# Hybrid trunk kernel: the modulation row products move into the feed-forwards and the projection

## The chip, the cores and the metric

One core of a Trainium2 chip runs the whole program. The metric is the device time of one execution in microseconds (us). In the trace an f32 matmul shows as two instructions (two LDWEIGHTS and two MATMUL), a float32r matmul and a transpose as one.

## The reference

Two trunk layers over three groups of 128 tokens (one of context, two of latents, all of width 1024):

```python
silu(c) @ w_ada + b_ada -> sh1, sc1, g1, sh2, sc2, g2, sh3, sc3, g3     # per layer, c and c_ctx
h = x * (1 + sc1) + sh1;  x = layer_norm(ALPHA * x + 0.5 * g1 * swiglu(h))
h = x * (1 + sc2) + sh2;  x = layer_norm(ALPHA * x + g2 * mixer(h))      # RWKV-7 | GLA | differential attention
h = x * (1 + sc3) + sh3;  x = layer_norm(ALPHA * x + 0.5 * g3 * swiglu(h))
```

The first line is what this change is about: for each of the three sub-layers a product of the two conditioning vectors with a 1024 x 3072 matrix (12 MB in f32). Two thirds of it (shift and scale) are needed as columns before the sub-layer's input can be made, the last third (gate) as rows before its output is added.

## The kernel before

The program is written by hand for each engine. SyncE streams all weights, in chunks of 128 x 2048 f32 (1 MB), through a ring of 6 slots; `arrived[slot]` says that a chunk landed, `used` that one was freed. A chunk of feed-forward or projection weights is two units: ScalarE rounds a unit to float32r (L1428), VectorE takes the rest (L1780), and TensorE makes three products for each (L850, L853, L854), moving 384 tokens.

A layer runs `turn_x(0)`, `feed_forward(0)`, `norm(0)`, `turn_x(1)`, `project`, attention, GLA and RWKV stages, `mix_out`, `norm(1)`, `turn_x(2)`, `feed_forward(2)`, `norm(2)`. Between layers and before the long mixer stages all engines meet, and at a layer's end the semaphores are cleared (L740, L741).

A feed-forward has 22 tiles. A tile is 24 matmuls for the gate half into bank 0, 24 for the up half into bank 1 (`tile_up`, L850 to L854), and 18 of 512 columns (`tile_down`, L896) into banks 2 to 7 for the tile ahead of it. Twenty of the tiles are in loops of four. `spread_gate` (L828) makes the gate as full tiles in banks 4 to 7, and ScalarE copies it (L1434).

The row products (`row_product`, L678) have silu(c) in 32 columns as the stationary operand and the weights as the moving one, 256 columns wide. The four pairs of k write to four groups of 32 partitions of the same bank. A set is 12 chunks: chunks 0 to 7 are shift and scale, 8 to 11 the gate. Sets 1, 2 and 3 (3 for the next layer) go through the ring like all weights. Set 1 is behind feed-forward 0, set 2 behind `mix_out`, set 3 behind feed-forward 2: `modulation_rows` makes 64 products under the norm, ScalarE copies them to `mod_row` (L715), 16 matmuls with `sel` (L699) turn them to columns, VectorE adds the biases (L722, L725), and only then `turn_x` can read the banks. The 32 gate products (`gate_rows`) stand between the transposes of `turn_x` (L842), or for set 3 behind the turns; VectorE adds them to `gate_row` (L733), which GpSimd has cleared and filled with the bias behind the norm (L2300, L2303).

In the norm VectorE's last operation is L1873; x is ready with its end. GpSimd loads the layer's parameters when a layer starts (L2339 to L2344).

## Time and profile before

| | before |
|---|---|
| three runs, us | 2279.59, 2276.31, 2273.07; median 2276.31 |
| profiled execution, us | 2282.56 |
| its span, us | 2280.8, mean granted clock 0.907 |
| TensorE busy | 2007.6 us (88%), 15488 matmul instructions |
| VectorE, ScalarE, GpSimd busy | 1109.6, 707.5, 120.0 us |
| HBM read | 269.56 MB, 120 GB/s over the span |
| row products (L678) | 1152 instructions |
| loads of a layer's start | 6 chunks of 1024 KB by SyncE; GpSimd: 626, 256, 736, 256, 256 and 1024 KB |

The span is cut by stages that repeat: turn phase, feed-forward, norm, turn phase, projection, mixer stages, output projection, norm, turn phase, feed-forward, norm; the first layer ends at about 1164, the second begins at about 1175. A stage in which TensorE is busy at every moment is read by its matmuls; at the seams the question is which engine's last instruction lets the next one go.

### The profile page before, as it was taken

The page shows a single profiled execution, that of the slowest core. Times are in us where ns is not written, and L with a number is a line of the kernel's source. Part 1 is how long each engine was busy: PE and PEld are TensorE (multiplying, and loading weights), DVE is VectorE, ACT ScalarE, POOL GpSimd, SP SyncE. Part 2 cuts the span into 40 slices and gives each one's busy share as a digit, 9 for nine tenths or more (in the row PEclk, how much of TensorE's full clock was granted, in tenths as well). Part 3 has the DMA queues.
Part 4 walks back from the last instruction along what each step waited for, and adds up shares of the span by engine and source line. Part 5 has one row for each costly group of instructions (what it writes and reads, how often), then busy time and mean ns, then how long its engine had stood idle before and what let it go on. Part 6 is the DMA issues. An engine that isn't in the chain of part 4 may idle for free. (4 is left out here: it accounts for less than half of the span.)

```text
span 2280.8 us, 36833 instructions
## 1 busy us (share of the span) xinstructions
PE 2007.6 (88%) x15488; PEld 1772.9 (78%) x15488; DVE 1109.6 (49%) x1687; ACT 707.5 (31%) x1155; POOL 120.0 (5%) x104
## 2 busy tenths in 40 slices
PE   5999998996749879999969999899966598899995
PEld 3899994985639759999849999769755596599995
DVE  0434335526784764343453434454377647634345
ACT  1422223335432333222232222143444223422221
POOL 0000001000022010000010000010000410100000
PEclk8899998998569989999969999989976699799998
DMA  7533336331000173333463333453300002733320
GB/s 323 218 127 129 129 122 247 117 123 47 12 1 4 50 273 124 127 115 126 151 241 129 126 129 129 167 202 120 129 6 7 2 4 90 264 129 129 121 100 28
DMA packets 40403, 274.65 MB, mean 120 GB/s; under 512 B 4741, under 2 KB 6549, under 8 KB 8289
## 3 DMA queue, kind: packets, MB, share of 16 engines
q1 hardware_dynamic: 35280, 255.34, 30.9%
q0 software_dynamic: 2400, 11.50, 1.3%
q10 hardware_dynamic: 2608, 6.14, 0.7%
q8 instruction: 89, 1.46, 0.3%
q14 instruction: 26, 0.20, 0.0%
HBM read 269.56 MB, written 3.41 MB: 120 GB/s over the span
## 5 line engine op out<-in xcount | busy, mean ns | idle before, releaser
L1780 DVE TENSOR_TENSOR ring_r<-ring,arena_r 128x1024 fp32r<-128x1024 f32 x280 | 327.6, 1221 | 658.5 <-ACT arena_r L1428 658.3
L854 PE MATMUL bank<-arena_r,ring_r 128*128 128x384 f32 x1728 | 588.0, 340 | 0.0
L850 PE MATMUL bank<-arena_r 128*128 128x384 f32 (+1 forms) x1504 | 520.2, 346 | 17.8 <-DVE arena_r L1800 12.9
L853 PE MATMUL bank<-arena_r 128*128 128x384 f32 x1408 | 476.3, 338 | 0.0
L854 PEld LDWEIGHTS bank<-arena_r,ring_r 128*128 128x128 f32 x1728 | 327.7, 190 | 0.0
L850 PEld LDWEIGHTS bank<-arena_r 128*128 128x128 f32 x1504 | 287.5, 191 | 29.3 <-DVE ring_r L1780 16.6
L896 PE MATMUL bank<-arena_r 128*128 128x512 f32 x1056 | 300.8, 393 | 0.0
L1428 ACT ACTIVATE arena_r<-ring 128x1024 fp32r<-128x1024 f32 x280 | 276.7, 1050 | 43.9 <-PE bank L854 31.0
L1467 ACT ACTIVATE arena<-bank 128x384 f32<-128x384 f32 x88 | 43.3, 492 | 757.5 <-PE bank L854 757.5
L853 PEld LDWEIGHTS bank<-arena_r 128*128 128x128 f32 x1408 | 266.2, 189 | 4.6 <-issue 1.0
L896 PEld LDWEIGHTS bank<-arena_r 128*128 128x128 f32 x1056 | 197.5, 188 | 38.3
L896 PE MATMUL bank<-ring_r,arena_r 128*128 128x512 f32 x528 | 164.5, 392 | 0.0
L678 PE MATMUL bank<-ring,silu_c 128*32 128x256 f32 x1152 | 100.8, 496 | 51.3 <-DVE arena L1836 29.2
L1780 DVE TENSOR_TENSOR ring_r<-ring,lnrow_r 128x1024 fp32r<-128x1024 f32 x60 | 73.4, 1226 | 147.3 <-ACT lnrow_r L1428 147.2
L896 PEld LDWEIGHTS bank<-ring_r,arena_r 128*128 128x128 f32 x528 | 99.3, 188 | 22.8
L850 PE MATMUL bank<-arena_r,lnrow_r 128*128 128x384 f32 x320 | 111.6, 349 | 4.1 <-DVE ring_r L1780 4.1
L678 PEld LDWEIGHTS bank<-ring,silu_c 128*32 128x32 f32 x1152 | 39.1, 135 | 97.5 <-DVE arena L1836 31.6
L853 PE MATMUL bank<-arena_r,lnrow_r 128*128 128x384 f32 x320 | 108.0, 337 | 0.0
L1428 ACT ACTIVATE lnrow_r<-ring 128x1024 fp32r<-128x1024 f32 x60 | 63.3, 1059 | 142.5 <-PE bank L854 142.5
L2298 POOL TENSOR_TENSOR x<-x,lnrow 128x1024 f32<-128x1024 f32 x12 | 28.2, 2347 | 1362.0 <-DVE x L1859 1362.0
L853 PE MATMUL bank<-ring_r,arena_r 128*128 128x512 f32 (+1 forms) x240 | 90.4, 377 | 0.0
L1037 PE MATMUL bank<-arena 32*128 32x128 f32 x384 | 52.1, 443 | 19.5 <-DVE arena L1984 19.1
(290 smaller groups left out, 2513.4 us busy)
## 6 DMA issues: line engine op xcount, KB each, us to landing
ring<-weights SPq DMA_DIRECT2D x230, 1024.0 KB, 4.8
ring<-first_ada SPq DMA_DIRECT2D x12, 1024.0 KB, 13.6
lnrow<-ln_in POOLq DMA_DIRECT2D x6, 1024.0 KB, 7.7
const<-consts ACTq DMA_DIRECT2D x1, 2659.0 KB, 13.7
x<-x_in ACTq DMA_DIRECT2D x1, 1536.0 KB, 19.5
y_out<-x SPq DMA_DIRECT2D x3, 512.0 KB, 2.6
rows<-row_in POOLq DMA_DIRECT2D x2, 736.0 KB, 14.5
par<-par_in POOLq DMA_DIRECT2D x2, 626.0 KB, 9.1
```

What stands on the lines that cost most here:

```text
L678: mm = pe.matmul(ps[q // 2][rows_at, (q % 2) * 256:(q % 2) * 256 + 256], silu_c[:, 2 * (k % 2):2 * (k % 2) + 32], ring_tile(n0 + q)[:, k, ...
L850: mm = pe.matmul(out, w_h, h_h, start=start, stop=False, skip_group_check=True)
L853: pe.matmul(out, w_h, h_l, start=False, stop=False, skip_group_check=True)
L854: return pe.matmul(out, w_l, h_h, start=False, stop=stop, skip_group_check=True)
L896: mm = pe.matmul(ps[2 + 2 * g + n][:, :], a, w[:, n * 512:n * 512 + 512], start=(first and a is a_hi and w is hi), stop=(last and a is a_l ...
L1037: mm = pe.matmul(ps[4 * (u % 2) + h][:, t], g_qk[lo:lo + GLA_DK, u % 2, 1, t], g_qk[lo:lo + GLA_DK, u % 2, 0, t], start=True, stop=True)
L1428: sc.activation(place, unit_of(FIRST[stretch], u), ACT.Copy).then_inc(w_rounded, 1)
L1467: sc.activation(sgt[:, b, :], ps[0][:, 0:TOK], ACT.Silu).then_inc(silu_done, 1)
L1780: ve.tensor_tensor(low_unit(FIRST[stretch], u), raw, place.bitcast(F32), ALU.subtract).then_inc(w_ready, 1)
L2298: po.tensor_tensor(x[:, g, :], x[:, g, :], lnrow[:, 1, :], ALU.add).then_inc(x_ready, 1)
```

## The change

1. Set 1 rides in feed-forward 0, set 3 in feed-forward 2 of the first layer. Each chunk is made as two halves of 128 columns (`half_row`): four of them in tile 1, one ahead of the gate half of each later tile, into free columns of bank 0. ScalarE copies each (`keep_row`). One turn (`turn_row`) stands ahead of each up half, four in tile 2, into free columns of bank 1. The gate part is no longer turned but added from `mod_row` in one operation at the feed-forward's end.
2. These chunks go to two slots of their own (`ada_ring`), loaded by GpSimd's queue from an array `ada_in` (`load_rows`), ahead of the norm in its order.
3. Set 2 rides in the projection, by the order `STREAM`: its chunks stay in the ring, one behind each chunk of weights from the second on (`row_part`), with two turns behind it (`turn_part`).
4. The feed-forward loops are written out; VectorE waits for the layer's parameters ahead of feed-forward 0; the gate's bias is fetched later or earlier by GpSimd (`next_gate`).
5. In attention's scores, in GLA's products, and in RWKV's `carries`, `gains` and `outer` the order of the matmuls is changed so that neighbours use other rows of the array and other banks; the waits ahead of `carries` and `gains` are joined.

The diff, cut to its core:

```diff
+def project_stream():
+    out, q = [("feat", 0)], 0
+    for c in range(1, N_FEAT):
+        out.append(("feat", c))
+        if q < 9:
+            out.append(("ada2", q))
+            q += 1
+    for c in range(N_TOKM):
+        out.append(("tokm", c))
+        if q < N_ADA:
+            out.append(("ada2", q))
+            q += 1
+    return out
...
+                    def half_row(j, i, bank, lo):
+                        n = N_ADA * (j // 2) + i // 2
+                        if i % 2 == 0:
+                            pe.wait_ge(ada_arrived[n % ADA_SLOTS], 16 * N_ADA * l + 16 * (n // ADA_SLOTS + 1))
+                        w = ada_ring[:, n % ADA_SLOTS, :].rearrange("p (k n) -> p k n", k=KT)
+                        for k in ROW_ORDER:
+                            rows_at = slice(32 * (k // 2), 32 * (k // 2) + 32)
+                            mm = pe.matmul(bank[rows_at, lo:lo + P], silu_c[:, 2 * (k % 2):2 * (k % 2) + 32],
+                                           w[:, k, P * (i % 2):P * (i % 2) + P], start=(k % 2 == 0), stop=(k % 2 == 1),
+                                           skip_group_check=True)
+                        mm.then_inc(mod_row_mm, 1)
+                    def turn_row(part, to, i):
+                        return pe.matmul(to[:, 2 * i:2 * i + 2], part, sel[:, :, 0], start=True, stop=True,
+                                         skip_group_check=True)
...
                             mm.then_inc(turned, 1)
-                            if j > 0:
-                                gate_rows(pe, FIRST[f"ada{j}"], range(4 * k, 4 * k + 4))
...
+                        def tile_up(f):
                             u = 0 if f == 0 else 3 * f - 1
+                            if i0 + f > 0:
+                                pe.wait_ge(silu_done, i0 + f)
+                            if rides and f >= 2:
+                                pe.wait_ge(mod_row_ready, rows0 + f + EARLY_HALVES - 2)
+                                half_row(j, f + EARLY_HALVES - 2, ps[0], TOK)
+                            widen(ps[0], u, gate_mm, fresh=(f == 0))
+                            if rides and f == 1:
+                                for i in range(EARLY_HALVES):
+                                    half_row(j, i, ps[2 + i // 2], P * (i % 2))
+                            if i0 + f > 0:
+                                pe.wait_ge(act_ready, i0 + f)
+                            if rides and f >= 2:
+                                if f == 2:
+                                    for i in range(EARLY_HALVES):
+                                        turn_row(mod_row[:, i * P:i * P + P], ps[1][:, TOK:TOK + 32], i)
+                                elif f + EARLY_HALVES - 3 < 16:
+                                    i = f + EARLY_HALVES - 3
+                                    mm = turn_row(mod_row[:, i * P:i * P + P], ps[1][:, TOK:TOK + 32], i)
+                                    if i == 15:
+                                        mm.then_inc(mods_done, 1)
+                            widen(ps[1], u + 1, up_mm)
...
+                        def row_part(q):
...
+                            for i, k in enumerate(ROW_ORDER):
+                                rows_at = slice(32 * (k // 2), 32 * (k // 2) + 32)
+                                mm = pe.matmul(bank[rows_at, lo:lo + 256], silu_c[:, 2 * (k % 2):2 * (k % 2) + 32],
+                                               ring_tile(n)[:, k, :], start=(k % 2 == 0), stop=(k % 2 == 1),
+                                               skip_group_check=True)
...
+                            if m == 0:
+                                pe.wait_ge(cond_ready, 2)
...
+                        for name, c in STREAM:
...
+                            else:
+                                if c == 0:
+                                    pe.wait_ge(gate_ready, 8)
+                                row_part(c)
+                                if 1 <= c <= 8:
+                                    turn_part(c - 1)
...
-                            for h in range(HEADS):
-                                for g in range(GROUPS):
+                            for g in range(GROUPS):
+                                for h in range(HEADS):
                                     lo, t = GLA_DK * h, slice(g * P, g * P + P)
...
-                    feed_forward(0)
-                    modulation_rows(pe, 1, FIRST["ada1"])
+                    feed_forward(0, True)
...
-                    modulation_rows(pe, 2, FIRST["ada2"])
                     turn_x(2)
-                    feed_forward(2)
-                    if not last:
-                        modulation_rows(pe, NMIX, FIRST["ada3"])
-                        gate_rows(pe, FIRST["ada3"], range(4 * KT))
+                    feed_forward(2, not last)
...
+                        if rides:
+                            ve.wait_ge(mod_row_ready, rows0 + HALVES)
+                            ve.wait_ge(gate_bias_loaded, 16 * NMIX * l + 16 * (j + 2))
+                            ve.tensor_tensor(gate_row[:, :], gate_row[:, :], mod_row[:, 2 * DM:3 * DM],
+                                             ALU.add).then_inc(gate_row_ready, 1)
...
+                    def load_rows(j):
+                        for n in range(N_ADA):
+                            slot = n % ADA_SLOTS
+                            if n == ADA_SLOTS:
+                                next_gate(j)
+                            if n >= ADA_SLOTS:
+                                po.wait_ge(mod_row_ready, row_base(j) + 2 * (n - ADA_SLOTS) + 2)
+                            po.dma_start(ada_ring[:, slot, :], ada_in[l, j // 2, n]).then_inc(ada_arrived[slot], 16)
```

TensorE's order, first place: in a riding feed-forward, from the end of one tile's down part over the next tile's gate half to the start of its up half. L850, L853, L854 (L870, L873, L874 in the changed kernel) are the three products of a wide step, L896 (L933) is the down part. Before:

```order
L896 MATMUL bank<-arena_r 128x512 x4
L896 MATMUL bank<-ring_r,arena_r 128x512 x2
L896 MATMUL bank<-arena_r 128x512 x2
...
L850 MATMUL bank<-arena_r 128x384
L853 MATMUL bank<-arena_r 128x384
...
L854 MATMUL bank<-arena_r,ring_r 128x384
...
L850 MATMUL bank<-arena_r 128x384
```

In the changed kernel (L833 is `half_row`, L840 `turn_row`):

```order
L933 MATMUL bank<-arena_r 128x512 x4
L933 MATMUL bank<-ring_r,arena_r 128x512 x2
L933 MATMUL bank<-arena_r 128x512 x2
L833 MATMUL bank<-arena,silu_c 32x128 x8
L870 MATMUL bank<-arena_r 128x384
L873 MATMUL bank<-arena_r 128x384
...
L874 MATMUL bank<-arena_r,ring_r 128x384
L840 MATMUL bank<-const,arena 128x2
L870 MATMUL bank<-arena_r 128x384
```

A burst of 8 matmuls to 32-column groups now stands ahead of the gate half, and a turn of one 128x128 block between gate half and up half.

Second place: TensorE from the end of feed-forward 0 to the projection (L925, in the changed kernel L994, is the first lora product). Before:

```order
L896 MATMUL bank<-arena_r 128x512 x2
L678 MATMUL bank<-ring,silu_c 32x256 x64
L699 MATMUL bank<-const,arena 128x2 x16
L842 MATMUL bank<-const,x 128x128 x3
L678 MATMUL bank<-ring,silu_c 32x256 x4
L842 MATMUL bank<-const,x 128x128 x3
L678 MATMUL bank<-ring,silu_c 32x256 x4
...
L678 MATMUL bank<-ring,silu_c 32x256 x4
L925 MATMUL bank<-arena,wad 64x384 x8
```

In the changed kernel (L864 is the transpose):

```order
L933 MATMUL bank<-ring_r,arena_r 128x512 x2
L933 MATMUL bank<-arena_r 128x512 x2
L864 MATMUL bank<-const,x 128x128 x24
L994 MATMUL bank<-arena,wad 64x384 x8
L870 MATMUL bank<-arena_r,lnrow_r 128x384
```

The 96 row products and 16 turns are gone from this place, and the 24 transposes stand in one piece.

## Rows read from the trace of the kernel before

**Rows 1.** Busy time by stretches; columns: stretch, length, TensorE busy (instructions), clock, DMA share, GB/s

```profile
91.00:341.00 250.00, 250.00 (x1315) 1.00 0.35 123
391.00:516.00 125.00, 125.00 (x660) 0.99 0.33 116
```

**Rows 2.** Chain of waits, feed-forward 2 of the second layer: start, duration, what

```profile
2222.16 4.17 PE bank L896 x18
2234.75 4.15 PE bank L896 x18
```

**Rows 3.** Timeline of TensorE, feed-forward 0 to projection, first layer

```profile
346.96 3.66 PE L678 MATMUL bank<-ring,silu_c 128*32 128x256 f32 x64
...
377.71 0.64 PE L678 MATMUL bank<-ring,silu_c 128*32 128x256 f32 x8
378.28 0.55 PE L842 MATMUL bank<-const,x 128*128 128x128 f32 x3
...
381.63 5.37 PE L925 MATMUL bank<-arena,wad 128*64 128x384 f32 x16
```

**Rows 4.** Timeline of VectorE, the same place

```profile
367.71 1.23 DVE L1873 TENSOR_TENSOR x<-x,lnrow 128x1024 f32<-128x1024 f32 x1
...
370.89 0.17 DVE L725 TENSOR_SCALAR cond<-cond 128x16 f32<-128x16 f32 x1
```

**Rows 5.** Timelines of VectorE, ScalarE and TensorE, end of layer 1, start of 2

```profile
1153.79 1.23 DVE L1873 TENSOR_TENSOR x<-x,lnrow 128x1024 f32<-128x1024 f32 x1
...
1163.21 0.69 DVE L733 TENSOR_TENSOR gate_row<-bank,gate_row 128x512 f32<-128x512 f32 x1 [1.26 <-PE bank L678]
...
1182.65 0.55 ACT L1448 ACTIVATE arena<-bank,cond 128x256 f32<-128x256 f32 x1
...
1175.00 1.53 PE L842 MATMUL bank<-const,x 128*128 128x128 f32 x6 [11.87 <-PEq L741]
...
1187.16 0.66 PE L850 MATMUL bank<-arena_r 128*128 128x384 f32 x1 [4.90 <-DVE arena_r L1800]
...
1197.98 3.59 PE L828 MATMUL bank<-gate_row,const 128*128 128x512 f32 x8
```

**Rows 6.** Timelines of VectorE and TensorE, mix-out to feed-forward 2, second layer

```profile
1955.95 1.23 DVE L1873 TENSOR_TENSOR x<-x,lnrow 128x1024 f32<-128x1024 f32 x1
...
1975.15 0.41 PE L850 MATMUL bank<-arena_r 128*128 128x384 f32 x1 [1.53 <-DVE arena_r L1800]
...
1983.64 3.59 PE L828 MATMUL bank<-gate_row,const 128*128 128x512 f32 x8
```

**Rows 7.** Timeline of TensorE, RWKV's carries

```profile
739.63 0.33 PE L1215 MATMUL bank<-arena 64*64 64x64 f32 x4
739.75 0.33 PE L1217 MATMUL bank<-arena 64*64 64x64 f32 x4
```

**Rows 8.** The row product's line: duration min/median/max, first and last start, forms

```profile
L678 PE MATMUL bank<-ring,silu_c x1152: 378/403/637, 6.2 to 1973.2; 128*32 128x256 f32 x192
```

**Rows 9.** The turns' line L699 in one microsecond: TensorE, weight load, clock, DMA, GB/s

```profile
364.80:365.80 1.00, 0.96 (x9) 0.96 (x9) 1.00 1.05 442
```

**Rows 10.** Busy time by stretches: turn phase of layer 2's start, and behind rows 3

```profile
1175.00:1182.30 7.30, 0.00 (x0) 0.00 (x0) 0.50 0.89 326
...
387.00:395.00 8.00, 5.97 (x25) 0.79 0.13 54
```

**Rows 11.** DMA issues at the second layer's start: KB, us to landing

```profile
lnrow<-ln_in POOLq DMA_DIRECT2D x1, 1024.0 KB, 23.0
...
arena<-vc_in POOLq DMA_DIRECT2D x1, 256.0 KB, 18.6
```

**Rows 12.** Timeline of TensorE, GLA's products

```profile
582.04 6.96 PE L1037 MATMUL bank<-arena 32*128 32x128 f32 x48 [1.81 <-DVE arena L1984]
```

**Rows 13.** Waits: total us, times, longest

```profile
DVE arena L1995 <- PE bank L1037: 7.5, 6, 2.2
...
DVE small L1926 <- PE bank L995: 4.2, 10, 0.8
```

More of the change, by code:

```diff
@@ L891, in tile_down @@
+                            widen(ps[1], u + 1, up_mm)
+                        def tile_down(f):
+                            hi, lo, free = unit(3 * f + 4 if f < FT - 1 else FFN_UNITS - 1)
+                            first, last = f == 0, f == FT - 1
+                            pe.wait_ge(act_split, i0 + f + 1)
+                            if rides and first:
+                                pe.wait_ge(mod_row_ready, rows0 + EARLY_HALVES)
                             for g in range(GROUPS):
@@ L1469, in feed_forward @@
                         for u in range(2, 5):
[L1470 to L1471 removed]
+                            round_unit(name, u, w_hi[:, u, :])
+                        silu(0)
                         gates(j)
[L1474 to L1479 removed]
@@ L2358, in _ @@
                     norm(1)
+                    if not last:
+                        load_rows(2)
                     norm(2)
```

426 lines of the change are left out of this document (235 added, 191 removed).

## The prediction

> **What bounds the kernel now.** I first read the busy time by stretches. Four stretches of 125 us and more, three in feed-forwards and one in a projection, have TensorE busy for their whole length at full clock (the first of the feed-forward ones and the projection's are shown) [rows 1]: what is added to TensorE there lengthens the program one for one. The chain of waits says the same in another way: the last matmuls of one feed-forward tile and of the next begin 12.58 us apart, and nothing but TensorE stands in the chain [rows 2]. So the three rides (feed-forward 0 of both layers, feed-forward 2 of the first) and the two projections are the worst places of the program for more matmuls.
>
> Then I read the five places that the rows are taken from, in order of time. At the end of the first feed-forward [rows 3] the first row products stand at 346.96, under VectorE's post-norm, whose last operation ends at 367.71 + 1.23 = 368.94 [rows 4]: they are hidden. What shows is the tail: the row turns (L699) and sums end 2.1 us after x is ready (L725 is over at 371.06), and the 32 gate products stand between the transposes. The reader is to see that most of what the change takes away there cost nothing. At the layer's end [rows 5] it did cost: the gate sums end at 1163.90, x was ready at 1155.02, and the meeting of all engines comes after both. At the second mix-to-feed-forward step [rows 6] x is ready at 1957.18 and the first wide matmul starts at 1975.15.
>
> **What the change adds to TensorE.** An f32 matmul shows as two instructions.
>
> Row products. 32 of them (64 instructions), 256 columns each, take 3.66 us at full clock [rows 3], 0.114 us apiece, so the 8 products of one chunk are 0.915 us. The ride cuts each chunk in two halves of 8 products with 128 columns: half of that is 0.46 us. The smallest matmuls of the trace, 64x64, begin 0.12 us apart for 4 instructions, 29 ns each [rows 7]; 16 of them are 0.47 us, so issuing does not forbid it. Each burst breaks the wide stream. In the first turn phase at full clock 4 products between transposes take 378.28 - 377.71 = 0.57 us [rows 3], and 4 x 0.114 = 0.46 without a break: 0.11 us for going to 32-column groups and back. A ride has 24 bursts: 24 x (0.46 + 0.11) = 13.7 us. The bounds of a burst: 0.46 (the break free) and 0.57 + 0.40 = 0.97, if one whole product (403 ns from start to end [rows 8]) must run out before the wide stream starts again. I take 0.57, as the nearest row has just this alternation.
>
> The Trainium skill has a rule against this edit: TensorEngine Tiling (Array Packing), Key Properties, says that changing the tiling mode drains TensorE. By it each burst would pay the drain; the trace agrees in kind, with the 0.11 us that stands ahead of this [rows 3].
>
> Row turns. At full clock 9 instructions fit into 1 us [rows 9], 0.22 us for one turn of two. A ride has 16, four together and twelve alone; alone I add half of the 0.11 above, 0.05: 4 x 0.22 + 12 x 0.27 = 4.1 us. A ride is 17.8 us, three are 53.5.
>
> Projection. 12 bursts of 256 columns, 12 x (0.915 + 0.11) = 12.3 us; 16 turns in 8 pairs, 3.5 + 0.4 = 3.9; and token unit 0 now waits for cond_ready, which VectorE can give only after the last turn: its two operations take 0.17 us or a little more each [rows 4], with hand-overs 0.7. That is 16.9 us, two are 33.8. Total added: 87 us. Low bound 64 (bursts and turns at the pace without breaks, turns hidden by half), high bound 138 (bursts at 0.97, turns at 0.36, one us of wait more per projection, 9 us of late loads).
>
> Costed at nothing: ScalarE's copies of the parts (24 per ride, 8 per projection; it is busy 31% of the span), VectorE's one addition of gate_row, which falls into its idle time before the norm, and VectorE's waits in the projection, which come behind the rest that TensorE needs next. The parameter wait now stands ahead of VectorE's feed-forward. The fifth parameter load lands 18.6 us after its issue [rows 11], at 1196.1, as the loads are issued from 1175.3 on, half a us apart; VectorE then has three rests, and TensorE's second tile needs the first of them, behind the gate spread that starts at 1197.98 and takes 3.6 [rows 5]: no wait. The unrolling of the loops costs TensorE nothing, as it had no gap at the loop's turn. In the loads of GpSimd, chunks 0 and 1 stand behind 3.2 MB of its own and beside 6 MB of the ring: the last of its loads landed 23.0 us after issue [rows 11], 1201.0. The 9.3 MB took from 1175.3 to then, 0.36 MB a us, so two MB more are 5.7 us, 1206.7, and the first half-row wants them at about 1205.5. Later chunks have some 25 us each. If the first are late, it is 1 to 3 us per ride.
>
> **What it takes away.**
> Layer end: 1163.90 - 1155.02 = 8.9 us [rows 5], in full.
> Mix-out to feed-forward 2. Without gate products the turn phase is the one of a layer's start: 1175.00 to 1183.20, 8.2 us [rows 5]; two of the first three transposes are already done when x is complete, so 7.7, and then 1.1 us to the first wide matmul. Before: 1975.15 - 1957.18 = 18.0 [rows 6]. Gain 9.1. But TensorE will have been idle through the norm, 22 us as from 346.96 to 368.94, and with transposes alone behind such a pause the granted clock stayed at 0.50 (1.2 GHz) in the layer start [rows 10]; there the first 48 wide matmuls took 1197.98 - 1187.16 = 10.8 us [rows 5]. Behind the turn phase with row products the clock was full and they took 1983.64 - 1975.15 = 8.5 [rows 6]. The change takes this warming away: -2.3. So 6.7 us, twice: 13.4.
> Feed-forward 0 to projection. The lora matmuls start at 381.63 [rows 3]; after, at 368.94 + 7.7 = 376.6, 5.0 earlier. They run partly cold (16 instructions, 5.4 us warm, about 2.5 more); before, the clock was down for a part behind them (0.79 in the mean [rows 10]). VectorE reaches its first weight rest earlier, as the gate sums (L733) are gone. I take 5 us, twice: 10.
> Sum 32, between 27 and 38.
>
> **The reorders** (scores, GLA, carries, gains, outer). In GLA 12 products of 32 rows take half of 6.96 us, 3.48 [rows 12]; all three token groups of one head use the same rows and bank, and the new order changes rows and bank at each. TensorE may fall to half. But VectorE waited for it only 7.5 us in both layers, and for the scores 4.2 [rows 13]. These are ceilings; I take 6 and 3. Carries, gains and outer already run at 29 ns an instruction [rows 7]: nothing. Sum 9, between 2 and 11.7.
>
> **Sum.** 87 - 32 - 9 = +46 us. The profiled execution took 2282.56 us for a span of 2280.8; it would be 2329. It lies 6.3 us above the median of the three runs, 2276.31; against the median I predict 2322.
>
> **The rivals.**
> *The breaks cost much more, or the loads come late.* Each burst costs 0.77 us, half way from 0.57 to 0.97, or GpSimd's chunks hold TensorE. For: 96 bursts inside float32r streams, a combination that no row shows. Against: rows 3. Price: 0.2 us x 72 = 14 us in rides, 5 in projections, 6 for turns, 9 for loads: 34 us more, +80, 2356. The late loads alone are 9 us of it, 2331, and have 0.04 of its chance.
> The skill's SBUF — State Buffer page, in its box on DVE blocking DMA, says that GpSimd can't write descriptors while VectorE runs some two-port operations; by it late loads become likelier. In no row of this trace is a GpSimd load issued during a feed-forward, so none shows it.
> *Slack in the wide stream takes the products: faster.* A tile takes 12.58 us for 48 matmuls of 384 columns and 18 of 512 [rows 2]; at 2.4 GHz these columns are 11.52 us. Over 22 tiles the slack is 23 us per feed-forward, more than a ride needs. If the bursts, also in the projection, only filled such slack, their price would be near nothing, and the gain of 41 us would stand: 2276 - 41 + 5 = 2240. It decides for measurably faster where the 87 us shrink below 34. For: the products are small in columns and rows. Against: the slack lies between single matmuls, the bursts stand in one piece, and 4 of them between transposes took their full time.
> *No difference.* The change adds at its low bound and takes away at its high one, 64 - 50 = 14, or a little less.
>
> **How the numbers follow.** Forecast (bursts at about 0.57 us, added 75 to 105 us): 0.64. More than that: 0.17. No difference: 0.06. Faster: 0.13. A measurement can tell 0.3%, 7 us. Slower 0.64 + 0.17 = 0.81. The range goes down to 2288, the low bounds of all costs with most of the gains, and up to 2368, past the dear rival; the faster case and no difference stay out below, with a little above.
>
> **What would show it.** Right: feed-forward tiles of 13.3 to 13.5 us in the rides against 12.58 in the last feed-forward, TensorE busy throughout, chain unchanged; projections 15 to 18 us longer; the meeting at the layer's end right behind x; the first 24 matmuls of feed-forward 2 at double duration. Wrong: tiles under 12.9 us (slack), tiles over 14 us (drains), TensorE waiting for DMA at half-rows, or a turn phase that is warm.

## The result, and the profile after

The changed kernel takes 2335.86 us (median of 4 runs, 2332.75 to 2337.73); the kernel before, run beside it, 2277.32 us (2273.07 to 2279.59, 4 runs). The ratio is 1.0258, with a 95% interval of 1.0238 to 1.0278: slower by 58.5 us. The forecast was 2322 with a range of 2288 to 2368. The profiled execution took 2336.76 us for a span of 2334.6, against 2280.8 before: 53.8 us more. The difference of the medians is larger because the profiled execution of before lay 5 us above its median, and that of after less than 1 us.

The span can be cut at places that both traces have: the first wide matmul of each feed-forward and projection, VectorE's first gated read of the accumulators in each norm (L1836 before, L1937 after), and TensorE's first operation behind the projection. The table gives the stretches between them, in us, first and second layer.

| Stretch | before | after | difference |
|---|---|---|---|
| feed-forward 0 (a ride) | 282.99 / 282.87 | 304.28 / 304.66 | +21.3 / +21.8 |
| norm to projection | 42.14 / 42.14 | 35.96 / 35.89 | -6.2 / -6.3 |
| projection | 132.13 / 132.14 | 149.21 / 149.18 | +17.1 / +17.0 |
| attention to mix-out | 291.32 / 290.81 | 283.31 / 285.57 | -8.0 / -5.2 |
| norm to feed-forward 2 | 39.91 / 40.03 | 32.59 / 32.59 | -7.3 / -7.4 |
| feed-forward 2 (a ride in the first layer alone) | 280.55 / 280.54 | 304.37 / 282.95 | +23.8 / +2.4 |
| norm to the second layer's first wide matmul | 54.22 | 45.41 | -8.8 |
| start and end of the program | 89.0 | 88.6 | -0.3 |

The differences add up to these 53.8 us within rounding. Busy time by stretches of the kernel after, with the columns of [rows 1]: a ride, the first projection, the feed-forward without a ride.

```profile
93.00:367.00 274.00, 274.00 (x1688) 1.00 0.42 149
424.00:543.00 119.00, 118.51 (x752) 1.00 0.58 212
...
2053.00:2309.00 256.00, 256.00 (x1340) 1.00 0.29 105
```

As before, TensorE has no gap in a feed-forward; it has some more instructions per us (1688 in 274 us, 1315 in 250 before), and every one of them lengthens the program. In the projection 0.5 us is idle.

Timeline of TensorE in the first ride (L933 is the down product, L833 the half-row product, L870 and L873 wide matmuls, L840 a row turn).

```profile
133.68 0.62 PE L933 MATMUL bank<-arena_r 128*128 128x512 f32 x2
134.23 0.64 PE L833 MATMUL bank<-arena,silu_c 128*32 128x128 f32 x16
134.81 0.44 PE L870 MATMUL bank<-arena_r 128*128 128x384 f32 x1
135.09 0.34 PE L873 MATMUL bank<-arena_r 128*128 128x384 f32 x1
...
139.12 0.28 PE L840 MATMUL bank<-const,arena 128*128 128x2 f32 x2
139.26 0.42 PE L870 MATMUL bank<-arena_r 128*128 128x384 f32 x1
```

In a stream without breaks a matmul of 512 columns begins 0.23 us behind the last one, and one of 384 columns 0.175. Here the second matmul of the first row begins at 133.91 and the burst at 134.23, 0.32 later; the eight products take 0.58; and between the first wide matmul (134.81) and the second (135.09) lie 0.28 us. So a burst costs 0.58 + 0.10 + 0.10 = 0.78 or 0.79 us, where the prediction had 0.57. A turn costs 0.14 to the next wide matmul and 0.07 behind it, 0.21 in all; four in one piece cost 0.81 and 0.08 behind them, 0.22 each. Tiles with both are 13.58 us long, tiles with the burst alone 13.37, tiles without a ride 12.58 [rows 2]. A ride: 20 bursts at 0.79 are 15.8, the first four in one piece 1.88 + 0.2, twelve turns at 0.21 and four together in 0.89 make 3.4: 21.3 us.

TensorE and VectorE in the projection, at the place where the first token unit waits for cond (L971 is a burst of 256 columns, L731 and L734 the sums).

```profile
504.45 1.07 PE L971 MATMUL bank<-ring,silu_c 128*32 128x256 f32 x16
505.45 0.61 PE L840 MATMUL bank<-const,arena 128*128 128x2 f32 x4
506.55 0.49 PE L870 MATMUL bank<-lnrow_r,arena_r 128*128 128x512 f32 x1 [0.49 <-DVE cond L734]
...
506.10 0.19 DVE L731 TENSOR_TENSOR cond<-bank,par 128x32 f32<-128x32 f32 x1 [3.38 <-PE bank L840]
506.32 0.17 DVE L734 TENSOR_SCALAR cond<-cond 128x16 f32<-128x16 f32 x1
```

The burst takes 1.00 us. A pair of turns takes 0.47 to the next wide matmul elsewhere; here, with the wait for cond, it is 1.10.

The seams: TensorE's first wide matmul behind a norm, and VectorE's last operation on x (L1974), for the projection, for feed-forward 2 of the first layer, and for the layer's end (L864 are the transposes; L1877 takes the rest of a weight unit, L1889 reads a transpose).

```profile
403.83 0.44 PE L870 MATMUL bank<-arena_r,lnrow_r 128*128 128x384 f32 x1
...
388.67 1.23 DVE L1974 TENSOR_TENSOR x<-x,lnrow 128x1024 f32<-128x1024 f32 x1
...
857.16 1.23 DVE L1974 TENSOR_TENSOR x<-x,lnrow 128x1024 f32<-128x1024 f32 x1
858.30 2.35 DVE L1877 TENSOR_TENSOR ring_r<-ring,arena_r 128x1024 fp32r<-128x1024 f32 x2
860.58 0.40 DVE L1889 TENSOR_SCALAR arena<-bank,cond 128x128 f32<-128x128 f32 x1
...
868.94 0.66 PE L870 MATMUL bank<-arena_r 128*128 128x384 f32 x1 [2.10 <-DVE arena_r L1898]
...
1194.10 1.23 DVE L1974 TENSOR_TENSOR x<-x,lnrow 128x1024 f32<-128x1024 f32 x1
...
1206.56 1.53 PE L864 MATMUL bank<-const,x 128*128 128x128 f32 x6 [33.29 <-PEq L749]
```

From x to the first wide matmul it is 403.83 - 389.90 = 13.9 us into the projection (20.1 before) and 868.94 - 858.39 = 10.6 into feed-forward 2 (17.9 before). Into feed-forward 2 VectorE takes the rests of two weight units (858.30, 2.35 us) before it reads the first transposes at 860.58; into the projection its first read is at 390.54, 0.64 us behind x. At the layer's end the transposes follow x after 11.2 us; before they did after 20.0.

Busy time by stretches at the second of these places: transposes, first 6 us of feed-forward 2, and behind.

```profile
852.50:868.90 16.40, 6.83 (x24) 0.50 0.48 192
868.90:875.00 6.10, 6.06 (x20) 0.52 0.00 0
875.00:880.00 5.00, 5.00 (x30) 1.00 0.01 3
```

The clock is at 0.50 in the whole turn phase and in the first 6 us behind it. The first 48 wide matmuls take 11.15 us in the first layer and 10.89 in the second, 8.50 and 8.49 before. This is the cold start that the prediction took 2.3 us for; it was 2.6 and 2.4.

Waits of the kernel after: total us, times, longest.

```profile
PEld bank L833 <- issue: 22.4, 63, 0.4
...
PE bank L833 <- DMA arena<-ada_in: 0.8, 1, 0.8
...
DVE arena L2113 <- PE bank L1127: 1.1, 2, 0.5
...
DVE small L2044 <- PE bank L1085: 4.8, 10, 1.0
```

Loads were late once: 0.81 us, at the first burst of the second layer. The 63 short waits of the half-row's weight loads (PEld), 0.36 us each, stand one ahead of each burst: its first weights go in with its first product, and not under the wide matmul ahead of it. VectorE's wait for GLA's products is down from 7.5 us to 1.1; its wait for the scores is 4.8, where it was 4.2 [rows 13].

### The profile page after: what moved, and what is told of

Its sections match the earlier page's. It is cut to its first block and busy times, and to the rows that moved or that the text cites. A ratio compares the mean times of both kernels' runs of the same rounds, so it can differ in the third digit from the quotient of the medians.

```text
span 2334.6 us, 37200 instructions
## 1 busy us (share of the span) xinstructions
PE 1968.3 (84%) x16064; PEld 1723.3 (74%) x16064; DVE 1107.1 (47%) x1688; ACT 714.1 (31%) x1223; POOL 139.3 (6%) x140
## 5 line engine op out<-in xcount | busy, mean ns | idle before, releaser
L1877 DVE TENSOR_TENSOR ring_r<-ring,arena_r 128x1024 fp32r<-128x1024 f32 x280 | 327.5, 1220 | 724.5 <-ACT arena_r L1515 714.5
L874 PE MATMUL bank<-arena_r,ring_r 128*128 128x384 f32 x1728 | 587.2, 340 | 0.0
L870 PE MATMUL bank<-arena_r 128*128 128x384 f32 (+1 forms) x1504 | 532.6, 354 | 18.8 <-DVE arena_r L1898 14.0
L873 PE MATMUL bank<-arena_r 128*128 128x384 f32 x1408 | 476.6, 339 | 0.0
L874 PEld LDWEIGHTS bank<-arena_r,ring_r 128*128 128x128 f32 x1728 | 327.7, 190 | 0.0
L870 PEld LDWEIGHTS bank<-arena_r 128*128 128x128 f32 x1504 | 287.2, 191 | 39.8 <-issue 18.4
L933 PE MATMUL bank<-arena_r 128*128 128x512 f32 x1056 | 300.8, 393 | 0.0
L873 PEld LDWEIGHTS bank<-arena_r 128*128 128x128 f32 x1408 | 267.9, 190 | 1.9 <-issue 1.0
L933 PEld LDWEIGHTS bank<-arena_r 128*128 128x128 f32 x1056 | 197.2, 188 | 38.8
L933 PE MATMUL bank<-ring_r,arena_r 128*128 128x512 f32 x528 | 164.6, 393 | 0.0
L1877 DVE TENSOR_TENSOR ring_r<-ring,lnrow_r 128x1024 fp32r<-128x1024 f32 x60 | 73.3, 1225 | 171.5 <-ACT lnrow_r L1515 171.4
L864 PE MATMUL bank<-const,x 128*128 128x128 f32 x144 | 39.3, 425 | 129.4 <-POOL x L2411 77.3
L864 PEld LDWEIGHTS bank<-const,x 128*128 128x128 f32 x144 | 24.2, 207 | 144.8 <-issue 70.0
L933 PEld LDWEIGHTS bank<-ring_r,arena_r 128*128 128x128 f32 x528 | 99.1, 188 | 23.4
L870 PE MATMUL bank<-arena_r,lnrow_r 128*128 128x384 f32 x320 | 111.5, 348 | 0.8 <-DVE ring_r L1877 0.8
L873 PE MATMUL bank<-arena_r,lnrow_r 128*128 128x384 f32 x320 | 106.6, 333 | 0.0
L873 PE MATMUL bank<-ring_r,arena_r 128*128 128x512 f32 (+1 forms) x240 | 90.1, 375 | 0.0
L870 PEld LDWEIGHTS bank<-arena_r,lnrow_r 128*128 128x128 f32 x320 | 59.9, 187 | 3.3 <-DVE ring_r L1877 2.0
```

The costliest lines, as they stand in the source:

```text
L864: mm = pe.transpose(bank[:, g * P:g * P + P], x[:, g, k * P:k * P + P], ident)
L870: mm = pe.matmul(out, w_h, h_h, start=start, stop=False, skip_group_check=True)
L873: pe.matmul(out, w_h, h_l, start=False, stop=False, skip_group_check=True)
L874: return pe.matmul(out, w_l, h_h, start=False, stop=stop, skip_group_check=True)
L933: mm = pe.matmul(ps[2 + 2 * g + n][:, :], a, w[:, n * 512:n * 512 + 512], start=(first and a is a_hi and w is hi), stop=(last and a is a_l ...
L1877: ve.tensor_tensor(low_unit(stretch, u), unit_of(stretch, u), place.bitcast(F32), ALU.subtract).then_inc(w_ready, 1)
```

## The experiments

Every time is a median, and the kernel before was run beside it on the same chip; its medians were 2277.2 to 2279.3 us. The stretches and waits are read from one profiled execution of each kernel.

**The new orders alone** (reorders, reorders_rwkv, gla_only). The kernel before, with all five orders, with those of RWKV only, and with this one only:

```
-                            for h in range(HEADS):
-                                for g in range(GROUPS):
+                            for g in range(GROUPS):
+                                for h in range(HEADS):
```

> The kernel before with only the five new orders of small products (scores, GLA, carries, gains, outer). Theory A: they are worth what the stretches between projection and norm lose in the two traces, 291.3 to 283.3 us in the first layer and 290.8 to 285.6 in the second, so 13 us: some 2264 us. Rival: only GLA and scores gain, as the prediction had it (9 us, 2268), and the rest of those stretches' loss belongs to the rides' other timing of the weight ring.

> The kernel before with only carries, gains and outer in the new order. Theory A: one instruction then takes about 18 ns in place of 29 and the stretch from the first carries to the norm is 3.4 and 2.2 us shorter in the two layers: 5.5 us, 2272. Rival, the prediction's own costing: these were limited by issue at 29 ns, so nothing, 2277.

> The kernel before with only the GLA products in the new order (token groups outside, heads inside). Theory A: the GLA stretch of each layer falls from 34.55 to 31.2 us as it does in the changed kernel, 6.7 us: 2271. All five orders together gave 9.7 us and the three of RWKV nothing, so 3 would be left for the scores. Rival: VectorE's wait in GLA moves to another place, and the five orders' gain comes from the scores: 2276.

All five: 2268.5 us, ratio 0.9957 (0.9940 to 0.9973), 9.7 us less. RWKV's three: 2278.2, ratio 1.0000 (0.9990 to 1.0011). GLA's alone: 2270.2, ratio 0.9966 (0.9952 to 0.9979), 7.7 us less by the ratio and 9.1 by the medians. So theory A falls for RWKV and holds for GLA. The intervals do not tell this from the 9.7 of all five, and the stretch of attention is 53.3 us in both layers before and 52.6 and 53.2 after, where the profiles of the other runs with the scores' new order have 52.3 to 53.8: what the scores' order gives is not shown. The 13.2 us that the stretch from attention to mix-out lost in the two traces are 9.7 of the orders and some 3 of scatter; with GLA's new order in all of them, this stretch was between 283.1 and 288.4 us in the profiles of the other runs.

In RWKV's carries the instructions did come closer together, which the prediction had ruled out. Busy time by stretches of one us within them, of the kernel before and of the changed one (x counts the instructions that are under way in the stretch):

```profile
740.00:741.00 1.00, 1.00 (x46) 1.00 0.00 0
```

```profile
767.00:768.00 1.00, 1.00 (x75) 1.00 0.06 16
```

75 instructions fall into a us that held 46 (66 begin in it, for 38), and the carries, gains and inner products together gained nothing: from the first of the carries to the first state step behind them it is 15.9 us before (739.63 to 755.49) and 15.8 after (766.92 to 782.75). TensorE is busy for 15.6 us of the first stretch and 12.2 of the second, so what its own work lost became idle time. VectorE and ScalarE are busy for 5.7 and 3.2 us of the second; that their steps in between set the pace is likely but not shown, and the edit also joined waits. The outer products behind, from the first state step to their end, took 7.4 to 8.5 us in the old order and 6.8 to 7.7 in the new, over all profiles: if that gain is real, under a us a layer, it is too small for the times of reorders_rwkv.

**Fewer and more breaks** (pairs, split). The bursts two by two, with the turns in the last tile; and each burst in two halves:

```
-                                half_row(j, f + EARLY_HALVES - 2, ps[0], TOK)
+                            if rides and f >= 2 and f % 2 == 0:
+                                half_row(j, f + EARLY_HALVES - 2, ps[0], TOK)
+                                half_row(j, f + EARLY_HALVES - 1, ps[1], TOK)
```

```
-                        for k in ROW_ORDER:
+                        for k in ROW_ORDER if part is None else ROW_ORDER[4 * part:4 * part + 4]:
...
+                                if mid is not None and k == KT // 2:
+                                    mid()
```

> The changed kernel, but in every ride the 20 single bursts go two and two (10 bursts of 16 products, the same products and columns), and the 16 turns stand together in the last tile. Theory A: a burst costs 0.79 us, of which some 0.2 lie at its two edges and some 0.15 in a start that does not grow with the columns (8 products of 128 columns take 0.58 us, of 256 columns 1.00). Ten fewer bursts per ride give 10 x 0.35 = 3.5 us, three rides 10.5: 2325. With the edges alone, 6 us: 2330. Rival: the price goes by the products only: 2336, the changed kernel's time.

> The changed kernel, but each of the 20 single bursts of a ride is cut in two of four products, the second in the middle of the gate matmuls (same products, same columns, 60 more breaks in the program). Theory A, from the run with paired bursts (30 breaks fewer took 1.8, 2.8 and 1.5 us off the three rides): a break costs 0.2 us at its edges and nothing grows with the count otherwise; tiles go from 13.58 to 13.8 us, three rides are 12 us longer: 2348. Theory B: four products between wide matmuls also overlap less among themselves, 0.15 us more per break: 2357. Rival: breaks are free and the price goes by products: 2336.

In pairs the second burst of a pair goes to bank 1, and waits for that bank too. Split does not compute the modulation rows rightly (why, the traces do not say), but it has the same products and columns. It took 2355.2 us, ratio 1.0338 (1.0320 to 1.0356): 19.4 us above the changed kernel for 60 breaks more, 0.32 us each. That is theory B. Timeline of TensorE in its first ride (L937 down, L871 and L874 wide):

```profile
132.33 0.63 PE L937 MATMUL bank<-arena_r 128*128 128x512 f32 x2
132.89 0.43 PE L833 MATMUL bank<-arena,silu_c 128*32 128x128 f32 x8
...
135.57 0.43 PE L833 MATMUL bank<-arena,silu_c 128*32 128x128 f32 x8
135.92 0.44 PE L871 MATMUL bank<-arena_r 128*128 128x384 f32 x1
```

Four products take 0.36 us where eight take 0.58, and the sixteen of a pair 1.01. So the first products of a burst carry about 0.14 us that does not grow with their number, beside the two edges of 0.10. What the 0.14 us are was not tried. A break is 0.34 us, and eight products of 128 columns are 0.44 us without it.

Pairs took 2331.9 us, ratio 1.0240 (1.0222 to 1.0257): 4.0 us less than the changed kernel, and not the 10.5 of theory A. Two tiles with a pair are 26.38 us long (the pairs start at 117.94 and 144.32) and 2 x 13.37 = 26.74 with single bursts: 0.36 us per break saved, as in split. Ten of them are 3.6 us per ride, but the rides are only 1.8, 2.8 and 1.5 us shorter. Part of it was given back at the end. Busy time by stretches of the pairs run, the 16 turns and the wide matmuls behind them:

```profile
346.90:350.40 3.50, 3.50 (x34) 1.00 0.08 33
350.40:354.50 4.10, 4.10 (x17) 0.62 0.00 0
```

The turns have two moving columns each. While 16 of them ran (3.5 us) TensorE counts as busy, and behind them the clock fell for 4 us: the next 24 wide matmuls took 5.8 us in place of 4.3; it was so in all three rides. With 0.1 us that the turns take longer in one piece, 2.0 of the 3.6 are left.

**What the edges belong to** (full_array). The products of the rides take the identity as the stationary operand, all 128 columns of it, so the modulation rows are not computed.

```
-                            mm = pe.matmul(bank[rows_at, lo:lo + P], silu_c[:, 2 * (k % 2):2 * (k % 2) + 32],
+                            mm = pe.matmul(bank[:, lo:lo + P], ident,
```

> The changed kernel, but the half-row products of the rides use a stationary of all 128 columns (the identity) in place of the 32-column one: the modulation rows of the rides are not computed. Theory A: the 0.2 us at the edges of a burst belongs to going from the whole array to 32-column tiles and back, as the turns (whole array, also f32, 0.14 us to the next wide matmul and 0.07 more behind it) show little of it. Then the gap from the last wide matmul to the first product falls from 0.33 to 0.23 us and that from the first wide matmul behind it to the second from 0.28 to 0.175, while the 8 products themselves take longer (16 instructions, about 0.09 us each as in the transposes, 1.5 us). Rival: the edges belong to going from float32r to f32; then both gaps stay.

Timeline of TensorE and its weight loads in the first ride (L933 down, L833 the product with the identity, L870 and L873 wide), and the weight loads of the same place of the changed kernel:

```profile
127.62 0.62 PE L933 MATMUL bank<-arena_r 128*128 128x512 f32 x2
128.09 1.95 PE L833 MATMUL bank<-arena,const 128*128 128x128 f32 x16
129.79 0.42 PE L870 MATMUL bank<-arena_r 128*128 128x384 f32 x1
130.04 0.34 PE L873 MATMUL bank<-arena_r 128*128 128x384 f32 x1
...
127.86 1.98 PEld L833 LDWEIGHTS bank<-arena,const 128*128 128x128 f32 x16
```

```profile
134.23 0.38 PEld L833 LDWEIGHTS bank<-arena,silu_c 128*32 128x32 f32 x16 [0.36 <-issue]
```

The products take 1.70 us, the run 2415.2 (one run). The first of them begins 0.23 us behind the last matmul of the down part (127.86), the step of the unbroken stream: the edge at the entry is gone. Its weights go in from 127.86 on, under that matmul; those of the 32-column burst began at 134.23, with its first product. Behind the burst 0.25 to 0.26 is left of 0.28, as behind a turn (139.52 - 139.26 = 0.26). So the entry edge comes with the 32-column tiles; the exit edge is mostly there with the whole array too. Theory A holds for the first and falls for the second. The change of the bank alone is not what is left: in the kernel before, the up half begins in a new bank 0.178 us behind the gate half, against 0.175 within them. The step from f32 to float32r remains, and was not tried by itself. The Trainium skill says in TensorEngine Tiling (Array Packing), Key Properties, that changing the tiling mode drains TensorE. The trace agrees, with 0.10 us at the entry.

**Keeping the clock up** (warm, warm_short). TensorE multiplies constants under the two norms within each layer of the changed kernel, where it was idle:

```
+                                    for _ in range(FILL[g]):
+                                        pe.matmul(ps[0][:, 0:TOK], ident, const[:, 0:TOK], start=True, stop=True)
```

> The changed kernel, but TensorE multiplies constants (f32, 384 columns, into a free bank; 36 matmuls before the first transpose of a turn phase behind a norm, 7 and 4 before the next two) where it was idle under the norm. Theory A: the loss of 2.6 and 2.4 us in the second feed-forwards and part of the turn phases' length come from the clock at 0.50 behind an idle TensorE. With the clock full, the first 48 wide matmuls take 8.5 in place of 11.1 and 10.9 us and the turn phases lose about 1.2 us each: 12 us less than the changed kernel or a little under, 2325. Rival: the idle stretch is not what lowers it (the clock falls again within the transposes), or the multiplications themselves run past the norm and hold the transposes back: 2336 or more.

> The run with filler matmuls again, with fewer of them (24, 5 and 3). In the first one an instruction took 0.30 us at full clock, the 94 of them 28 us, and the norm is 22 us long: the transposes began 7 us late, but the clock stayed at 1.00 and the first 48 wide matmuls took 8.50 us. Now 24 x 0.6 = 14.4 us end before the first group of x is ready, and 5 and 3 fill the gaps behind it (3.5 and 2.3 us). Theory A (the clock is lowered by the idle stretch, and that costs): the steps into feed-forward 2 and its first 48 matmuls together 3 to 4 us shorter than in the changed kernel, twice, the step into the projection 1 to 2 us, twice: 8 to 12 us, 2326. Rival: what stands there is bound by VectorE's and ScalarE's reading of the transposes, and only the 48 matmuls gain: 5 us, 2331.

Warm took 2357.9 us, ratio 1.0356 (1.0336 to 1.0375), as its rival had it: the filler ran past x, and the steps into projection and feed-forward 2 were 43.1 and 38.1 us long, 7.1 and 5.5 more than in the changed kernel. Its first 48 wide matmuls in feed-forward 2 took 8.50 us in the first layer, as before the change, and 10.04 in the second, where the clock fell to 0.50 just behind the first of them. Busy time by stretches, first layer:

```profile
880.80:889.20 8.40, 8.40 (x48) 1.00 0.01 2
```

Warm_short took 2335.4 us, ratio 1.0244 (1.0223 to 1.0266), the changed kernel's time within the scatter. The two steps into the projection were 1.6 us shorter, those into feed-forward 2 0.4, and the 48 matmuls took 10.3 and 9.9 us (first layer):

```profile
868.10:878.40 10.30, 10.28 (x48) 0.81 0.01 2
```

So the low clock followed TensorE's idling, and its price, 2.65 us where filler kept the clock up, is near the 2.3 predicted. But filler under the norm alone helps little: in warm_short's first layer the clock fell at 861.9, behind a wait of TensorE of 2.4 us between its transposes (858.7 to 861.1), in which VectorE does the two weight rests. The 5 to 6 us that these places gained do not show in the time: the stretches from attention to mix-out, which vary by as much from profile to profile, were 3 us longer in both layers than in the changed kernel.

**All products under the norm** (under_norm). The kernel before with the new orders and other waits:

```
                 if j > 0 and q == 4:
-                    pe.wait_ge(acc_read, j)
+                    pe.wait_ge(acc_read, GROUPS * (j - 1) + 1)
...
                     modulation_rows(pe, 1, FIRST["ada1"])
+                    gate_rows(pe, FIRST["ada1"], range(4 * KT))
```

> The kernel before with the new orders, and no rides: all 96 products of a set run while VectorE does the norm (each pair of banks as soon as VectorE has read it, the gate products behind the turns), the copies lie between ScalarE's norm steps, and VectorE's gate sums stand in the next turn phase. Theory A: the seams gain what they gain in the changed kernel (6.2 us twice, 7.3 twice, 8.8 once, less 5 for the cold start of feed-forward 2: 31 us) without any of the 98 us that the rides and projections pay; with 13 us for the orders that is 44 less than before, 2233. Rival: the ring's 12 chunks do not arrive within the norm's 22 us, TensorE holds the transposes back, and no more than 15 us are left beyond the orders: 2250 or above.

2251.1 us, ratio 0.9887 (0.9870 to 0.9904): 27 us less than before and 85 less than the changed kernel. Beyond the orders it is 17 us, not 31: nearer the rival. Busy time by stretches in the step into the projection (the first products, the turns), and waits in the step into feed-forward 2, both of the first layer:

```profile
346.20:350.00 3.80, 3.79 (x72) 1.00 0.68 231
358.40:366.20 7.80, 7.80 (x44) 0.50 1.00 423
...
ACT arena_r L1434 <- DMA ring<-weights: 7.0, 1, 7.0
...
PE bank L678 <- DMA ring<-weights: 4.4, 3, 2.0
```

The ring brings a chunk in 2.5 us at 423 GB/s, TensorE waits 4.1 and 4.4 us for chunks in the two steps. Into the projection the last products of the rows end 13 us into the norm, the turns behind them run at the 0.50 clock, to which it fell right after a wait of 2.8 us for a chunk, and the gate products end 3 us after x. Into feed-forward 2 ScalarE waits 7 us for the first weights. The layer's end is 7.6 us shorter than before: there nothing else is behind x.

**The additions of the norm** (vector_adds). In the rows of under_norm, GpSimd adds the offset to two token groups, and VectorE works beside it:

```profile
359.92 2.35 POOL L2311 TENSOR_TENSOR x<-x,lnrow 128x1024 f32<-128x1024 f32 x1 [280.36 <-DVE x L1865]
363.50 2.35 POOL L2311 TENSOR_TENSOR x<-x,lnrow 128x1024 f32<-128x1024 f32 x1 [1.23 <-DVE x L1865]
...
360.50 1.78 DVE L1860 SCALAR_TENSOR_TENSOR small<-small 128x1 f32<-128x1 f32 x1
...
363.60 3.33 DVE L1865 TENSOR_TENSOR x<-x,lnrow 128x1024 f32<-128x1024 f32 x1 [0.18 <-ACT x L1500]
```

An operation on one column that takes 0.16 us elsewhere takes 1.78 and ends with GpSimd's first addition (362.28 and 362.27); one of 1.22 takes 3.33 and ends 1.08 behind the end of the second.

```
+                        def offset(g):
+                            ve.wait_ge(scaled, GROUPS * j + g + 1)
+                            ve.tensor_tensor(x[:, g, :], x[:, g, :], lnrow[:, 1, :], ALU.add).then_inc(x_ready, 1)
```

> The kernel with all products under the norm, and in each norm VectorE adds the offset row to the first two token groups itself, in place of GpSimd. In the traces a VectorE operation of 0.16 us takes 2.33 and one of 1.22 takes 3.33 when it starts beside GpSimd's addition. Theory A: VectorE loses 2.2 and 2.1 us to GpSimd and pays 1.2 for an addition of its own, so each of the six norms is 1.8 us shorter, 11 us in all, less what the loads of the ring then hold back at the two steps into feed-forward 2: 2240 to 2244. Rival: the loads of the ring set the end of the seams anyway, so the time is that of the run with products under the norm, 2251.

2244.9 us, ratio 0.9873 (0.9845 to 0.9901). The interval overlaps that of under_norm, so the 6.2 us between them are not shown by the times. VectorE's rows of this run:

```profile
358.39 0.16 DVE L1860 SCALAR_TENSOR_TENSOR small<-small 128x1 f32<-128x1 f32 x1
358.98 1.23 DVE L1865 TENSOR_TENSOR x<-x,lnrow 128x1024 f32<-128x1024 f32 x1 [0.43 <-ACT x L1500]
360.24 1.22 DVE L1869 TENSOR_TENSOR x<-x,lnrow 128x1024 f32<-128x1024 f32 x1
```

x is complete 20.5 us behind the norm's start, in place of 22.05 (20.0 to 21.1 in the other norms), and the end of the program, where nothing covers it, is 23.05 us in place of 25.07. In the inner seams the products are then last, and those steps are no shorter as a whole: 40.2 and 40.5 us into the projection, where under_norm has 39.1 and 40.2. The Trainium skill's page SBUF — State Buffer, Who interferes with whom, says that a VectorE instruction with two SBUF inputs contends with a GpSimd instruction that reads SBUF; these rows agree.

**The gate products behind the transposes** (gates_behind, gates_mixed). The edit is against vector_adds.

```
-                    gate_rows(pe, FIRST["ada1"], range(4 * KT))
                     pe.wait_ge(par_loaded, 16 * LAYER_DMAS * l + 16 * LAYER_DMAS)
                     turn_x(1)
+                    gate_rows(pe, FIRST["ada1"], range(4 * KT))
```

> The run with VectorE's own additions, and the gate products of the two inner sets moved behind the eight transpose groups, where TensorE waits for the split of h. In the run before this one x was complete at 363.86 and TensorE still turned rows and multiplied gate products until 369.88. Theory A: the transposes start 6 us sooner, the 64 instructions run warm (3.7 us) while VectorE and ScalarE split h, and each inner seam is 3 to 5 us shorter: 16 us, 2229. Rival: the first weights of the next stretch land late, because four chunks of the ring are held by the gate products for longer, and the seams stay: 2245.

> The run with VectorE's own additions, with the gate products behind the transposes at the step into the projection alone; at the step into feed-forward 2 they stay ahead of them. In the run with both moved the step into the projection lost 3.4 us in each layer, the step into feed-forward 2 gained 3.8 and 4.5 us with its first weight chunk held back. Theory A: the two places are independent, so 6.9 us less than the run with the additions (2245): 2238. Rival: the moved products only shift the ring's loads, and the next stretch gives it back: 2244.

Moved at both inner seams: 2244.1 us, ratio 0.9851 (0.9834 to 0.9867). The steps into the projection were 36.8 and 37.0 us, 3.4 and 3.5 less than in vector_adds, those into feed-forward 2 were 38.3 and 38.7, 3.8 and 4.5 more: there ScalarE waits 7.8 us for the first weight chunk (first layer), and its reads of the transposes stand behind that in its order, so TensorE waits 6.9 us between transposes. In vector_adds ScalarE waits 7.5 us too, but the gate products fill that time; in gates_behind they follow the transposes and end 0.3 us ahead of the first wide matmul. Moved at the projection alone: 2241.3 us, ratio 0.9844 (0.9824 to 0.9864), the lowest median of all, 38 us below before; the steps were 37.1 and 37.8, and 34.5 and 35.6. Between the last three runs the intervals tell no difference.

## Why the prediction was right

**The sign and the sum.** TensorE's wide stream was the bound, and what was put into it lengthened the program one for one. Added 98.4 us (predicted 87, between 64 and 138), taken away 36.0 less 5.0 for the cold starts, 31.0 (predicted 32), orders 9.7 by the runs (predicted 9): 57.7, and the medians differ by 58.5. The forecast was +46: sign, place and gains were right, and what is missing is almost all in one term.

**Row products in a ride** are the term that was too small: 0.57 us a burst, measured 0.79. The step that failed is the nearest row: the products between transposes [rows 3] gave 0.11 us for a break, and the wide stream pays 0.34 (0.10 + 0.10 at the edges, 0.14 at the start). There the stream itself was broken up by the transposes, so its rows could not show what a break costs an unbroken one. The 0.46 for the products themselves was right (0.44). Over 60 single bursts it is 13 us; the turns gave 2.0 back, and the three rides were 10.8 us longer than forecast. The prediction's dear rival put the burst at 0.77, near the measured one by its number alone: it is half way between two bounds. It was dear by 34 us because it added costs that did not come: late loads 9 (0.8), turns 6 (below zero). The high bound of 138 us does not come out of the costs given with it: they add up to 136, or to 143 with the dear break in the projections too.

**Row turns**: 4.1 us a ride, measured 3.4. The half of a break that was added for a lone turn is not there: alone 0.21, in fours 0.22.

**Projection**: 16.9, measured 17.1 and 17.0, and that is luck: its terms cancel. Twelve bursts cost 12.0 us and about 2.3 at the edges (predicted 12.3 for both), the turns 3.7 (3.9), the wait 0.6 (0.7); and 1.5 us came back, which no term had, as the first 24 matmuls take 4.3 us at full clock where they took 5.9 before.

**Layer end**: 8.9, measured 8.8. **Into feed-forward 2**: 9.1 less 2.3, measured 7.3 and 7.4 less 2.6 and 2.4. The wide matmul follows x after 10.6 us, not 8.8. The cold transposes were in the 8.8, as they were read from a cold turn phase, and the 1.1 from ScalarE's last read to the wide matmul came as said (1.15). What was left out are the two weight rests that VectorE takes ahead of its first read, 2.35 us: the four turn groups took 9.4 us from x, not 7.7. **Into the projection**: 5, measured 6.2 and 6.3. VectorE has no such rests there, and the lora matmuls start 6.9 us behind x (7.7 forecast). They cost 1.7 us more in the cold (2.5), and the 2.0 us that the first wide matmul waited for a weight rest before are gone.

**The orders**: GLA 6, measured 7.7 (by the medians 9.1) by its run and 6.4 by VectorE's wait; scores 3, not shown; RWKV nothing, and it was nothing, though not for the reason given: the issue at 29 ns was no floor, and the instructions go at 1.6 times the old rate.

**Costed at nothing**: the loads by GpSimd (0.8 us in the whole program), ScalarE's copies, the parameter wait and the unrolled loops. All of that held. The page that the prediction named for late loads (the Trainium skill's SBUF — State Buffer, box on DVE blocking DMA) did not decide here: the 36 loads landed in a median of 5.3 us, beside VectorE's work in the feed-forwards. Whether any of that was of the kind that the page names, the traces do not say.

**The rivals.** No slack in the wide stream took the products: the faster case falls, as every tile grew by what was put in. Of the tests that the prediction gave, 13.58 us lies a little over the 13.3 to 13.5 for a tile with burst and turn; TensorE busy throughout and the meeting right behind x came as said. The first 24 matmuls of feed-forward 2 took 6.9 us for 4.3, somewhat less than double. The chain of waits in a ride is not shown: that of the changed kernel reaches back to 1708 us only, and no ride lies between there and the end.

## What to carry to other kernels

Small work in the stream of the engine that is the bound costs its own time and a price per break (here 0.34 us against 0.44 for the work itself), so it belongs into time that the engine idles anyway, or into few and long pieces. Here the idle time was in the norm: splitting one wait on the accumulators into three and freeing one bias row earlier let most of the same products run there, and with the new orders that is 85 us faster than the changed kernel, which has them too. A price for a break is taken from a row in which the same stream is broken, not from one in which small operations alternate already. And what another engine does first behind the last operation of a stage belongs into the count of a seam: here two weight rests made some 1.6 us.

## What was not expected

Sixteen row turns in a row, with TensorE busy throughout, were followed by 4 us at a clock of 0.62 in the mean; twelve lone turns between wide matmuls cost no clock. (In under_norm the turns themselves ran at 0.50, but there the clock had fallen before them, behind a wait for a chunk.) VectorE loses 1.6 and 2.1 us to two additions of GpSimd that would cost it 1.22 each. And ordering small products so that neighbours use different row halves brought 75 instructions into a us for 46, where the prediction had taken 29 ns an instruction for a floor of issue; yet it saved no time.
